# Last two weight slots interleaved by output chunk, a third weight buffer, and sums of chunks added on GpSimd

## What is computed

```python
def conv_ffn(x, norm_g, w_up, conv_w, conv_b, w_down):
    h = rms_norm(x, norm_g)
    u = causal_dwconv(h @ w_up, conv_w, conv_b)
    gate, val = jnp.split(u, 2, axis=-1)
    return x + (jax.nn.silu(gate) * val) @ w_down
...
        proj = h @ w_in[l]
...
        h = layer_norm_2(DEEPNORM_ALPHA * h + mixed @ w_out[l], ln1_g[l], ln1_b[l])
        ff = jnp.square(jax.nn.relu(h @ w_up[l])) @ w_down[l]
        h = layer_norm_2(DEEPNORM_ALPHA * h + ff, ln2_g[l], ln2_b[l])
```

## Time and profile before

| | |
|---|---|
| median of 3 runs | 2584.38 us (2579.65 to 2585.29) |
| profiled execution | 2579.82 us |
| its span | 2578.1 us |
| mean granted TensorE clock | 0.982 |
| TensorE (PE) busy | 2450.6 us, 95% |
| VectorE (DVE) busy | 1415.4 us, 55% |
| ScalarE (ACT) busy | 1080.4 us, 42% |
| GpSimd (POOL) busy | 51.9 us, 2% |

### The profile page before, as it was taken

One profiled execution on the slowest core, in us unless ns is written; L12 is line 12 of the kernel. 1 busy time (PEld: TensorE's weight loads), 2 busy tenths in 40 slices (PEclk: granted clock), 3 DMA queues, 4 the chain that ended last, 5 costly groups with the idle time before them and its releaser, 6 DMA issues.

```text
span 2578.1 us, 33411 instructions
## 1 busy us (share of the span) xinstructions
PE 2450.6 (95%) x11814; PEld 1932.8 (75%) x11814; DVE 1415.4 (55%) x2298; ACT 1080.4 (42%) x1633; POOL 51.9 (2%) x64
## 2 busy tenths in 40 slices
PE   8989999999998999998988989999989899899997
PEld 6667888887776788886866668888858666788885
DVE  5876777336673777724457664244264774533424
ACT  4534444236883544413545443233154543432322
POOL 0000000000000000000012000000000200000000
PEclk9999999999999999999999999999999989999998
DMA  4212333321212233333211123333322112233331
GB/s 172 62 45 86 94 97 98 98 89 58 73 57 66 83 96 98 98 98 119 66 50 42 50 65 98 98 91 97 97 86 67 41 34 74 65 98 98 98 98 65
DMA packets 57422, 210.38 MB, mean 82 GB/s; under 512 B 6478, under 2 KB 6880, under 8 KB 56960
## 3 DMA queue, kind: packets, MB, share of 16 engines
q1 hardware_dynamic: 56736, 204.51, 25.6%
q0 software_dynamic: 608, 4.81, 0.5%
HBM read 207.20 MB, written 2.10 MB: 81 GB/s over the span
## 4 chain that ended last, share of the span: by engine, by line
PE 82%; DVE 9%; ACT 4%; issue 3%; DVEq 1%; DMA 0%; ACTq 0%
PE PS L1076 14%; PE PS L1077 14%; PE PS L1078 14%; PE PS L1090 10%; PE PS L1092 10%; PE PS L1091 10%; PE PS L1111 2%; DVE PB L1890 2%; PE PS L1249 1%; ACT PB L713 1%; DVE RSTD L1662 1%; PE PS L1241 1%; PE PS L1102 1%; DVE CONV L1731 1%; PE PS L1127 1%
## 5 line engine op out<-in xcount | busy, mean ns | idle before, releaser
L1639 DVE TENSOR_TENSOR WL<-RAW,WH 128x1024 fp32r<-128x1024 f32 x376 | 462.3, 1229 | 652.8 <-ACT WH L554 652.2
L554 ACT ACTIVATE WH<-RAW 128x1024 fp32r<-128x1024 f32 x376 | 397.5, 1057 | 825.3 <-PE PS L1092 559.1
L1076 PE MATMUL PS<-HH,WH 128*128 128x512 f32 x1792 | 708.8, 396 | 4.8 <-DVE KR L1898 2.9
L1077 PE MATMUL PS<-HL,WH 128*128 128x512 f32 x1792 | 699.0, 390 | 0.0
L1078 PE MATMUL PS<-HH,WL 128*128 128x512 f32 x1792 | 698.9, 390 | 0.0
L1076 PEld LDWEIGHTS PS<-HH,WH 128*128 128x128 f32 x1792 | 337.2, 188 | 81.2 <-issue 6.7
L1077 PEld LDWEIGHTS PS<-HL,WH 128*128 128x128 f32 x1792 | 337.5, 188 | 71.2 <-issue 3.3
L1078 PEld LDWEIGHTS PS<-HH,WL 128*128 128x128 f32 x1792 | 337.2, 188 | 71.1
L1092 PE MATMUL PS<-MH,WL 128*128 (+1 forms) x864 | 336.1, 389 | 0.0
L1090 PE MATMUL PS<-MH,WH 128*128 (+1 forms) x864 | 336.1, 389 | 0.0
L1091 PE MATMUL PS<-ML,WH 128*128 (+1 forms) x864 | 336.1, 389 | 0.0
(11 more groups left out here) (275 smaller groups left out, 2544.0 us busy)
## 6 DMA issues: line engine op xcount, KB each, us to landing
RAW<-wstream SPq DMA_DIRECT2D x376, 512.0 KB, 3.6
W<-cmp_w POOLq DMA_DIRECT2D x2, 2048.0 KB, 8.7
X<-xt SPq DMA_DIRECT2D x4, 512.0 KB, 5.6
out<-X SPq DMA_DIRECT2D x8, 256.0 KB, 2.0
TAB<-tables SPq DMA_DIRECT2D x1, 1871.5 KB, 12.7
WS<-spatial_w SPq DMA_DIRECT2D x1, 512.0 KB, 8.5
BS<-spatial_b SPq DMA_DIRECT2D x1, 256.0 KB, 8.6
PW<-pool_w POOLq DMA_DIRECT2D x2, 128.0 KB, 2.3
```

The costliest lines, as they stand in the source:

```text
L554: act.activation(WH[:, b, :], RAW[:, b, :], ACT.Copy).then_inc(w_hi, 1)
L1076: pe.matmul(PS[:, bank, :], WH[:, b, w], HH[:, k, :], start=(k == 0), stop=False)
L1077: pe.matmul(PS[:, bank, :], WH[:, b, w], HL[:, k, :], start=False, stop=False)
L1639: dve.tensor_tensor(WL[:, b, :], RAW[:, b, :], WH[:, b, :].bitcast(F32), ALU.subtract).then_inc(w_lo, 1)
```

## The change

It has five parts.

1. `add_pair`: before every norm (eight times; the first halves of the square blocks keep the old form) the last two slots are used together. For each output chunk the three matmuls of slot 6 and the three of slot 7 follow one another, so bank n is complete after 6(n + 1) of 48 matmuls. One wait stands ahead of all, for both slots' low parts.
2. WX, a third buffer with a high and a low part: `early_hi` and `early_lo` put the slot after the pair there, and `first_tiles` takes its first tile from it. WX lies on memory that the blocks use otherwise, so GpSimd's loads of the mixer's weights now wait for that tile.
3. `first_tiles` waits for HH, multiplies WH and WL with it, and then waits for HL.
4. `fold` on GpSimd adds the eight squares (six in "final") or the first six chunks of X (into MU). Ones-products: one for a norm of the first kind instead of eight, three instead of six in "final", three and eight instead of six and six in a layer norm. The squares of the gated blocks have a buffer of their own, SQF.
5. `centre` in the layer norms reads the sum from PSUM, without the mean in between.

```diff
+LAYER_NORMS = [f"ln{a}_{l}" for l in range(DEPTH2) for a in (1, 2)]
+FOLD = 6
...
+        with ExitStack() as early:
+            sb("FILLW", [P, EARLY_FILL], scope=early)
+            WX = sb("WX", [P, 2, D], F32R, scope=early)
...
         def _(pool):
+            def fold(dst, src, last, ready, base, nm):
+
+                for n in range(1, last + 1):
+                    pool.wait_ge(ready, base + n + 1)
+                    ins = pool.tensor_tensor(dst, src[:, 0, :] if n == 1 else dst, src[:, n, :], ALU.add)
+                    if n < last:
+                        pool.drain()
+                ins.then_inc(n_part, 1)
...
-                pool.wait_ge(tile_done, L_IN[l])
+                pool.wait_ge(tile_done, L_IN[l] + 1)
...
+            def early_hi(s):
+
+                act.wait_ge(w_loaded[0], 16 * (s // 2 + 1))
+                if s:
+                    act.wait_ge(tile_done, s - 2)
+                act.activation(WX[:, 0, :], RAW[:, 0, :], ACT.Copy).then_inc(w_hi, 1)
...
+                    if n == DC - 2 and gain == "ffn_norm_g0":
+                        act.wait_ge(tile_done, F_UP[0])
...
-            for k in range(4, DC + 1):
+            for k in range(4, DC):
                 split_hi(0, E_OUT + k)
+            early_hi(F_UP[0])
...
+            def add_pair(i, rows):
+
+                pe.wait_ge(w_lo, 2 * i + 2)
+                for n in range(DC):
+                    w = slice(n * P, (n + 1) * P)
+                    for b, (rh, rl) in enumerate(rows):
+                        pe.matmul(PS[:, n, :], WH[:, b, w], rh, start=False, stop=False)
+                        pe.matmul(PS[:, n, :], WH[:, b, w], rl, start=False, stop=False)
+                        last = pe.matmul(PS[:, n, :], WL[:, b, w], rh, start=False, stop=(b == 1))
+                        if n == DC - 1:
+                            last.then_inc(tile_done, 1)
+                        elif b:
+                            last.then_inc(y_done, 1)
...
+            def sum_folded(buf, nm):
+
+                pe.wait_ge(n_part, PART[nm])
+                pe.matmul(PS[:, 2, :], tab("ones"), buf[:, 0, :], start=True, stop=True).then_inc(n_sum, 1)
+
+            def sum_rest(bank, folded, buf, ready, base, nm, done):
+
+                for n in range(FOLD, DC):
+                    if n == DC - 1:
+                        pe.wait_ge(n_part, PART[nm])
+                        pe.matmul(PS[:, bank, :], tab("ones"), folded, start=False, stop=False)
+                    pe.wait_ge(ready, base + n + 1)
+                    last = pe.matmul(PS[:, bank, :], tab("ones"), buf[:, n, :], start=(n == FOLD), stop=(n == DC - 1))
+                last.then_inc(done, 1)
...
+                        wh, wl = first_weights(b, slice(k * P, (k + 1) * P))
+                        pe.wait_ge(h_hi, fill + k + 1)
+                        pe.matmul(PS[:, b, :], wh, HH[:, k, :], start=(k == 0), stop=False)
+                        pe.matmul(PS[:, b, :], wl, HH[:, k, :], start=False, stop=False)
                         pe.wait_ge(h_lo, fill + k + 1)
...
-            for k in range(DC):
+            for k in range(DC - 2):
                 pe.wait_ge(h_lo, H_FILL["even_out"] + k + 1)
...
+            pe.wait_ge(h_lo, H_FILL["even_out"] + DC)
+            add_pair((E_OUT + DC - 2) // 2, [(HH[:, k, :], HL[:, k, :]) for k in (DC - 2, DC - 1)])
...
             def layer_norm(nm):
...
+                sum_rest(0, MU[:], X, x_ready, XR[nm], nm, n_add)
+                for n in range(DC):
+                    sum_squares(NB2, n, 3, nm, n == DC - 1)
...
-                mean(0, D, n_add, ADD[nm] + FIRST + 1)
-                centre(X, range(DC))
-                squares_part(NB2, FIRST, nm)
+                dve.wait_ge(n_add, ADD[nm])
+                for n in range(DC):
+                    dve.scalar_tensor_tensor(X[:, n, :], PS[:, 0, :], -1.0 / D, X[:, n, :], ALU.mult, ALU.add).then_inc(n_cent, 1)
```

More of the change, by code:

```diff
@@ L1053, in square_ffn @@
                             act.activation(MH2[:, bass.ds(2 * i + b, 1), :], SB[:, b, :], ACT.Copy).then_inc(q_hi, 1)
-                    last = l == DEPTH2 - 1 and half == 1
-                    with act.Fori(1, F2H // 2 + (0 if last else 1)) as i:
+                    with act.Fori(1, F2H // 2) as i:
                         for b in range(2):
                             split_hi((up + F2H) // 2 + i, b)
+                    if not half:
+                        split_hi(0, up + 2 * F2H)
+                        split_hi(0, up + 2 * F2H + 1)
+                    elif l < DEPTH2 - 1:
+                        early_hi(L_IN[l + 1])
+                        split_hi(0, L_IN[l + 1] + 1)
             for l in range(DEPTH2):
@@ L1095, in add_rows, with sum_rows, sum_squares @@
                 last.then_inc(tile_done, 1)
-            def sum_rows(buf, bank, waits, done, part=None):
+            def add_pair(i, rows):
[10 more added lines that the diff above has]
+                            last.then_inc(y_done, 1)
+            def sum_rows(buf, bank, waits, done):
                 for q, (n, *wait) in enumerate(waits):
                     pe.wait_ge(*wait)
[L1102 to L1110, removed]
+                    pe.matmul(PS[:, bank, :], tab("ones"), buf[:, n, :], start=(q == 0), stop=(q == len(waits) - 1))\
+                      .then_inc(done, 1)
+            def sum_squares(buf, n, bank, nm, final):
+                pe.wait_ge(n_sq, NORM[nm][0] + n + 1)
                 last = pe.matmul(PS[:, bank, :], tab("ones"), buf[:, n, :], start=(n == 0), stop=final)
@@ L1210, in conv_ffn @@
                         add_rows(down + i, b, MH[:, bass.ds(k, 1), :], ML[:, bass.ds(k, 1), :], False, False)
[L1211 to L1214, removed]
+                pe.wait_ge(f_mlo, FC * (l + 1))
+                add_pair(down + FC // 2 - 1, [(MH[:, k, :], ML[:, k, :]) for k in (FC - 2, FC - 1)])
             conv_ffn(0)
@@ L1620, in square_ffn @@
                             add_rows(down + i, b, MH2[:, bass.ds(k, 1), :], ML2[:, bass.ds(k, 1), :], False, False)
+                    if half:
+                        pe.wait_ge(q_lo, done + F2H)
+                        add_pair(down + F2H // 2 - 1, [(MH2[:, k, :], ML2[:, k, :]) for k in (F2H - 2, F2H - 1)])
+                        continue
                     for b in range(2):
@@ L1798, in _ @@
                 low(Y, HC + n, H_FILL["even_out"])
[L1799 removed]
+            for k in range(4, DC):
                 split_lo(0, E_OUT + k)
+            early_lo(F_UP[0])
             dve.wait_ge(r_loaded, 32)
```

123 lines of the change are left out of this document (65 added, 58 removed).

## The result

The changed kernel takes **2589.97 us** (median of 7 runs, 2586.84 to 2592.28), the kernel before 2579.65 (7 runs beside it, 2577.83 to 2585.29). The ratio is 1.0039, 95% interval 1.0028 to 1.0049: slower by 0.4%, some 10 us, more than the 0.2% that can be told from no change. The three runs of before that the prediction had seen (2579.65 to 2585.29) had a median 4.7 above that of the seven.

The account below looks back on a forecast made before the run. TensorE, busy 95% of the span, was taken as the bound: only its waits or vain work matter. Losses of 34.6 us against gains of 30.7 gave +3.9 on the 2584.38 median: 2588.3 us, range 2576 to 2597.

Parts of the forecast that it names:

- the sum (+3.9): Whole kernel: losses of 34.6 us against gains of 30.7, net +3.9.
- the base (2584.38): Median of three runs of the kernel before, in us, on which the predicted difference was put.
- The pair's pause: At eight pairs, TensorE waits 2.7 us for the second slot's low part: +21.6 us.
- The clock: Behind ten new TensorE pauses, each costs 0 or 1.8 us by a lower clock; half of ten taken, +9.0 us.
- the clock falls at nearly every new pause: Rival, at each pair's first products: five more falls of 1.8 us, 2597 us; chance 0.17.
- Turns on GpSimd and VectorE: Gated blocks and attention: GpSimd adds and VectorE low parts exclude each other, some 1.85 us per chunk; gains 5.4, 5.4, 4.5.
- The start: First norm: seven adds taking turns with eight low parts, square root at 22.5 us, no gain (0).
- freedom from turns: Rival, GpSimd and VectorE don't exclude each other: start 4.1 us less, blocks 1.3 + 1.3 + 0.6, 2581 us; chance 0.13.
- Final and layer norms: Last weight product to square root: 3.1 us in the final norm (-2.2), 11.4 in four layer norms (-11.2 together).
- HH before HL: At four norms that fill HH anew, TensorE starts earlier, between 0 and 0.75 us each; 0.5 taken, -2.0 us.
- Mixer's weights: Two mixers: loads on GpSimd's queue wait for the first tile, so TensorE waits 2.0 us each, +4.0 us.
- Third buffer: Slot loaded into WX after each pair: nothing waits for it, 0.

Follow-up runs that it names:

- run 1: Changed kernel, but the pair waits for the second slot's low part only ahead of that slot's first product: 2585.0 us, ratio 1.0017 to the kernel before.
- run 2: Changed kernel, but the pair's second slot runs three chunks behind the first: 2573.9 us, ratio 0.9977 to the kernel before.
- run 5: Changed kernel, but TensorE repeats twelve products while the pair's second slot is made ready: 2582.5 us, ratio 1.0006 to the kernel before.
- run 3: Changed kernel, but the last two slots run one after the other (second eight chunks behind): 2597.7 us, ratio 1.0076 to the kernel before.
- run 6: Changed kernel, but GpSimd adds only two of eight squares at the start, gated blocks and attention: 2585.7 us, ratio 1.0024 to the kernel before.
- run 4: Changed kernel, but the gate weights GW count on a semaphore of their own: 2583.4 us, ratio 1.0010 to the kernel before.
- run 7: Kernel before, with only the last two slots interleaved three chunks apart, two weight buffers, no adds on GpSimd: 2604.5 us, ratio 1.0089.
- run 10: Changed kernel with the pair three chunks apart and the gate weights' own semaphore, all eight squares folded: 2560.8 us, ratio 0.9921 to the kernel before.
- run 9: Changed kernel once more, unaltered, one execution for a second profile: 2599.3 us.
- run 8: Changed kernel, pair three chunks apart, gate weights' own semaphore, six squares folded ahead of gated blocks and attention: 2562.3 us, ratio 0.9927 to the kernel before.

## Why the prediction was right or wrong

The time of 2588.3 lies 1.7 from the measured median, and the range holds it, but that is partly luck: the sum (+3.9) was 6 too small, and the base (2584.38) 4.7 too large. On the side I was wrong: I gave "the same" 0.46 and "slower" 0.34, and it is slower by 0.4%.

- *The pair's pause, 21.6:* right, 21.8, by 2.71 to 2.72 each, ended by WL. Runs 1 and 2 show that it is the wait for the second slot and that it can be hidden.
- *The clock, "each pause costs 0 or 1.8; I take half of ten":* **this step failed.** The size was nearly right (1.6 for 1.8), the share was not: seven of the eight pairs, and the first mixer's pause on top, 14.4 with the rest of the mixers where the sum has 9.0. The earlier trace rows were pauses of 2.4 us with two falls in four, too few to set a share on. The rival "the clock falls at nearly every new pause" describes the pairs. Its 2597 was too high because its base was 4.7 too high and because it counted ten falls of 1.8, 18.0 where 14.4 were measured. Run 5 shows the cause.
- *Turns on GpSimd and VectorE:* right in mechanism and size: STD at T + 8.0 and 7.3 at the gated blocks, predicted 7.8, and at T + 8.1 ahead of the attention, predicted 8.6; reciprocal of the attention at T + 10.9, predicted 11.5. The Trainium skill ("SBUF — State Buffer", who interferes with whom) says that a VectorE instruction with two SBUF inputs contends with a GpSimd instruction that reads SBUF, and one with a single SBUF input does not. The rows agree: HL and WL, with two SBUF operands, grew from 0.75 to 1.57 and (run 3) from 1.23 to 2.17, and X<-X,PS, with one, stayed at 0.67. The start: 22.33, predicted 22.5; run 6 gained 4.0 there, which looks like the 4.1 that I gave to freedom from turns, but only some 1.8 of it is that (run 6). What I had wrong is one add by itself: 1.4 us to the next, not 1.2. That changed nothing in the changed kernel, where the pause covers the adds, and made runs 2 and 3 worse than I expected.
- *Final and layer norms:* right: STD at T + 3.2 (3.1) and T + 11.4 (11.4), gains of 2.2 and 11.4.
- *HH before HL, 2.0:* mis-sized; 0.45 at each square block and nothing seen at the mixers, 0.9.
- *Mixer's weights, 2.0 each:* 2.63 and 1.66 more than before, right in the sum (4.3). Run 4 shows that only the shared semaphore makes TensorE wait.
- *Third buffer, 0:* right for what it costs, but I missed what it is for (run 7): VectorE's order would otherwise hold every residual add until the pair's first slot has ended.

So the change holds some 30 us of gains in the norms, and gives them back, and 10 more: 34 at the entrance to them and 7 in the mixers. With the entrance mended (run 10) it is some 20 us faster than the kernel before.

## What to carry to other kernels

When two steps that share a double buffer are interleaved, the second one's preparation comes out into the open: reckon its full length. Start the first one ahead by as many chunks as that takes, and give the step after the pair a buffer of its own. Price each new idle stretch of TensorE of about 2 us or more in a busy stretch with the fall of its clock behind it (here 1.6 us, in 34 of 40), and if it can't be removed, fill it. Sums moved to an engine with slow adds pay only when their inputs arrive spread out; and a semaphore that several transfers share makes the smallest wait for the largest.

## What was not expected of the hardware

- At an idle stretch of 1.94 us the clock fell as often (6 of 8) as at 2.72 in run 4 (6 of 8). With TensorE kept busy on repeated products it fell at none.
- The falls in the mixers' attention stand in different places in two profiles of the same program (run 9), and kernels with the same work there differ by up to 8 us in that part (runs 8 and 10). Which pauses lead to a fall there stays open; profiles of single runs should be compared stage by stage, and small edits by many runs.
- GpSimd's add of 128x512 is shown as 1.29 to 1.30 and repeats every 1.4 us beside X<-X,PS; the 1.06 of the earlier trace rows, of 128x525, was a bad price for it, and the 1.30 of the other row there, of 128x513, the right one.
